# Four expert tiles with homes of their own beside the ring, and two block buffers in place of four

## The reference, cut to what matters

```python
def hier_moe(h, w_rg, b_rg, w_re, b_re, w1, w3, w2):
    ...
    slot_tok = jnp.zeros(n_blocks * MOE_BLOCK, jnp.int32).at[dest].set((order // TOP_K).astype(jnp.int32))
    ...
    xs = h[slot_tok].reshape(n_blocks, MOE_BLOCK, d_)

    def run(args):
        xb, e = args
        return (jax.nn.silu(xb @ w1[e]) * (xb @ w3[e])) @ w2[e]

    ys = lax.map(run, (xs, block_e)).reshape(-1, d_)
    return jnp.zeros_like(h).at[slot_tok].add(ys * slot_gate[:, None])
```

## Time and profile before

| | us |
|---|---|
| median of 3 runs | 2305.1 (2302.08 to 2305.42) |
| profiled execution | 2304.22 |
| its span | 2302.4 |
| PE busy | 2035.6 |
| DVE busy | 786.6 |
| ACT busy | 457.2 |
| POOL busy | 189.7 |

### The profile page before, as it was taken

How to read it: one execution, slowest core, us unless ns; L and a number is a source line. 1 busy time by engine, 2 the same in 40 slices (tenths; PEclk the granted TensorE clock), 3 DMA queues, 4 the chain that set the end, 5 groups by cost and what they waited for, 6 DMA issues and landing times.

```text
span 2302.4 us, 30476 instructions
## 1 busy us (share of the span) xinstructions
PE 2035.6 (88%) x11971; PEld 1212.3 (53%) x11972; DVE 786.6 (34%) x1836; ACT 457.2 (20%) x1059; POOL 189.7 (8%) x240
## 2 busy tenths in 40 slices
PE   6999999799877789999877777798999999999998
PEld 4566566444433335757433333344875575775574
DVE  1355674111111116656111111114466312456413
ACT  2142112111111112411111111111123212123112
POOL 1000001111111110001111111111000000000000
PEclk9999999999999999999999999999999999999999
DMA  9235649999999985686999999996343332343230
GB/s 376 110 129 240 255 156 378 423 426 427 427 425 426 425 345 211 236 317 257 424 425 425 424 425 425 427 420 242 134 182 129 111 147 110 147 165 129 95 142 19
DMA packets 62872, 640.95 MB, mean 278 GB/s; under 512 B 15868, under 2 KB 16420, under 8 KB 24240
## 3 DMA queue, kind: packets, MB, share of 16 engines
q1 hardware_dynamic: 41728, 588.39, 61.9%
q0 software_dynamic: 19984, 44.74, 5.5%
q10 hardware_dynamic: 1056, 6.37, 0.7%
HBM read 622.50 MB, written 44.17 MB: 290 GB/s over the span
## 4 chain that ended last, share of the span: by engine, by line
PE 62%; DMA 31%; DVE 4%; ACT 2%; issue 1%; SPq 0%; POOL 0%; DVEq 0%
DMA ring<-in_moe 26%; PE ps L866 10%; PE ps L1037 10%; PE ps L519 8%; PE ps L1051 6%; PE ps L1148 5%; PE ps L507 3%; PE ps L695 3%; DMA ring<-in_denseA 3%; PE ps L1220 2%; PE ps L872 2%; PE ps L1016 2%; PE ps L541 2%; PE ps L771 2%; PE ps L584 1%; DMA ring<-in_denseB 1%
## 5 line engine op out<-in xcount | busy, mean ns | idle before, releaser
L866 PE MATMUL ps<-ring,scr 128*64 128x256 f32 (+1 forms) x4800 | 667.5, 430 | 178.2 <-DMA ring<-in_moe 169.3
L866 PEld LDWEIGHTS ps<-ring,scr 128*64 128x64 f32 x4800 | 333.4, 138 | 485.9 <-DMA ring<-in_moe 239.3
L1833 DVE TENSOR_TENSOR scr<-ps,scr 128x512 f32<-128x512 f32 (+3 forms) x98 | 54.6, 558 | 574.6 <-PE ps L866 487.0
L1037 PE MATMUL ps<-ring,hT 128*128 128x512 f32 (+1 forms) x576 | 245.5, 578 | 5.1 <-ACT hT L1546 5.1
L519 PE MATMUL ps<-ring,hT 128*128 128x512 f32 (+1 forms) x512 | 199.3, 547 | 0.5 <-ACT hT L1516 0.5
L1444 POOL DMA_INDIRECT ys_scratch<-scr,ytab x128 | 125.0, 976 | 825.4 <-DVE scr L2495 791.6
L1670 ACT ACTIVATE scr<-ps 128x512 f32<-128x512 f32 x64 | 38.2, 597 | 760.8 <-PE ps L866 694.0
L2495 DVE COPY scr<-ps 128x1024 f32<-128x1024 f32 x64 | 78.4, 1224 | 269.3 <-PE ps L866 243.4
L1037 PEld LDWEIGHTS ps<-ring,hT 128*128 128x128 f32 x576 | 108.1, 193 | 117.8 <-issue 108.2
L1516 ACT ACTIVATE scr<-ps 128x256 f32<-128x256 f32 (+2 forms) x168 | 71.3, 436 | 403.7 <-PE ps L507 403.7
L519 PEld LDWEIGHTS ps<-ring,hT 128*128 128x128 f32 x512 | 97.3, 193 | 93.0 <-issue 89.2
(11 more groups left out here) (330 smaller groups left out, 2019.2 us busy)
## 6 DMA issues: line engine op xcount, KB each, us to landing
ring<-in_moe SPq DMA_DIRECT2D x192, 2048.0 KB, 15.9
ring<-in_denseB SPq DMA_DIRECT2D x48, 2048.0 KB, 7.7
ring<-in_denseA SPq DMA_DIRECT2D x36, 2048.0 KB, 16.2
scr<-ys_scratch POOLq DMA_DIRECT2D x6, 1024.0 KB, 7.2
modB<-mod_scratch POOLq DMA_DIRECT2D x10, 512.0 KB, 11.3
ring<-kv_scratch SPq DMA_DIRECT2D x2, 2048.0 KB, 8.6
tok_scratch<-hb POOLq DMA_DIRECT2D x6, 512.0 KB, 2.9
memT_scratch<-modB ACTq DMA_DIRECT2D x2, 1024.0 KB, 6.7
```

The costliest lines, as they stand in the source:

```text
L866: last = mm(out, lhs(c)[:, 0:64], w(c)[:, half * q:half * (q + 1)], start=(c == 0), stop=(c == n - 1))
L1037: last = mm(T["open"][:, 0:cols], hT16[:, c, t * P:(t + 1) * P], w[:, c, 0:cols], start=(c == 0), stop=(c == DC - 1))
L1833: return V.tensor_tensor(out, a, b, op)
```

## The change

Four expert tiles no longer pass through the ring. `ASIDE` lists their places: 3 in the first layer; 3, 7 and 10 in the second. Each has a home in memory that is idle at the time, in two halves of 1 MB that are loaded by two DMAs (`load_aside`). The others move up in the ring (`in_ring`), and SP's written-out part is one turn of its loop longer. In the first layer SP issues the aside tile after places 0 and 1 and after waits for the last router product's bank (`routed`), the modulation rows (rows_out) and the four writes of tokens (tok_out). In the second layer place 3 is issued ahead of place 0 (its wait, `turned`, is on transposes of the attention stage) and places 7 and 10 after `routed` and rows_out. The homes take half of `hb`, so the blocks have two buffers: gather k waits for block k - 2. In the second layer `xs_lo` and `xs_hi` are laid out for four blocks and not eight. PE's products and their order are the same; for an aside tile PE waits on its own semaphore.

```diff
-XS_W = SLOT_BLOCKS[0] * P + P
+XS_W = tuple(n * P + P for n in SLOT_BLOCKS)
+
+ASIDE = ((3,), (3, 7, 10))
...
-    xs_lo = hT[:, 0:3 * XS_W].rearrange("p (c t) -> p c t", c=3)
+    xs_lo = [hT[:, 0:3 * w].rearrange("p (c t) -> p c t", c=3) for w in XS_W]
...
-    xs_hi = cv(5, XS_W)
+    xs_flat = cv(5 * XS_W[0])
+    xs_hi = [xs_flat[:, 0:5 * w].rearrange("p (c t) -> p c t", c=5) for w in XS_W]
...
+    half_tile = TILE // 2
+
+    low_mod, low_rows = (v[:, 2:4, :].rearrange("p a b -> p (a b)") for v in (modB, hb))
+    aside = (((low_mod, low_rows),),
+             ((S[:, 2:4, :].rearrange("p a b -> p (a b)"), low_rows), (low_mod, hT[:, half_tile:2 * half_tile]),
+              (scr[:, 10400:10400 + half_tile], scr[:, 10400 + half_tile:10400 + 2 * half_tile])))
...
+    aside_in = [[sem(f"aside_in{l}_{j}") for j in ASIDE[l]] for l in range(DEPTH)]
...
-    SEG_M = 3 * E + 2
+    SEG_M = [3 * E + 2 - len(a) for a in ASIDE]
...
+    def in_ring(l, at):
+
+        return baseM[l] + at - sum(a < at for a in ASIDE[l])
+
     for l in range(DEPTH):
         for b in range(E):
             for k, s in enumerate((m_h1, m_h3, m_y)):
-                released[baseM[l] + place(b, k)] = (s, blocks_before[l] + b + 1)
+                if place(b, k) not in ASIDE[l]:
+                    released[in_ring(l, place(b, k))] = (s, blocks_before[l] + b + 1)
+    free_when = {}
...
+            free_when["turned", l] = (tp_full, T["tp"])
...
             route(nt - 1, 2)
+            free_when["routed", l] = (acc_free, T["acc"])
...
-                                                   hb[:, k % 4, c * P:(c + 1) * P], ident)
+                                                   hb[:, k % 2, c * P:(c + 1) * P], ident)
...
-            def moe_tile(i, q):
-
+            def moe_tile(i, at, width):
+
+                if type(i) is int and at in ASIDE[l]:
+                    n = ASIDE[l].index(at)
+                    pe.wait_ge(aside_in[l][n], 32)
+                    per = half_tile // width
+                    return lambda c: aside[l][n][c // per][:, c % per * width:(c % per + 1) * width]
+                q = in_ring(l, at) if type(i) is int else baseM[l] + at - len(ASIDE[l])
...
+            def load_aside(n):
+
+                src = d["moe"][l][tile_of(*in_order[ASIDE[l][n]])]
+                for k in range(2):
+                    sp_.dma_start(aside[l][n][k], src[:, k * half_tile:(k + 1) * half_tile]).then_inc(aside_in[l][n], 16)
+
+            def expert_tile(at):
+
+                dense(lambda i: d["moe"][l][tile_of(*in_order[at])], 1, in_ring(l, at))
+
+            if l > 0:
+                sp_.wait_ge(*free_when["turned", l])
+                load_aside(0)
+            expert_tile(0)
+            expert_tile(1)
+            sp_.wait_ge(*free_when["routed", l])
+            sp_.wait_ge(rows_out, (96, 144)[l])
+            if l == 0:
+                sp_.wait_ge(tok_out, 16 * 4)
+                load_aside(0)
+            else:
+                load_aside(1)
+                load_aside(2)
+            for at in range(2, 6 * UNROLL - 1):
+                if at not in ASIDE[l]:
+                    expert_tile(at)
+            with sp_.Fori(1, E // UNROLL - 1) as i:
...
-                if k >= 4:
-                    pool.wait_ge(rows_T, 2 * (K0 + k - 3))
-                pool.indirect_dma_start(hb[:, k % 4, :], None, tok_d,
+                if k >= 2:
+                    pool.wait_ge(rows_T, 2 * (K0 + k - 1))
+                pool.indirect_dma_start(hb[:, k % 2, :], None, tok_d,
```

More of the change, by code:

```diff
@@ L219, in program @@
     assert cv.at <= 4096, cv.at
+    half_tile = TILE // 2
[3 more added lines that the diff above has]
+              (scr[:, 10400:10400 + half_tile], scr[:, 10400 + half_tile:10400 + 2 * half_tile])))
+    assert 3 * XS_W[1] <= half_tile and 7168 + 5 * XS_W[1] <= 10400
     keys_new = lnB[:, :, :].rearrange("p a b -> p (a b)")
@@ L403, in program @@
         baseM.append(g)
-        g += SEG_M
+        g += SEG_M[l]
     for l in range(DEPTH):
@@ L815, in _ @@
             memory_keys(8 * DC - T["keys"])
-            B0, G0 = blocks_before[l], baseM[l]
+            B0 = blocks_before[l]
             pe.wait_ge(acc_free, T["acc"])
@@ L896, in work @@
                 def work(is_wide):
-                    w = moe_tile(i, G0 + (3 * u - 1 + k if u > 0 or type(i) is not int else k))
-                    products(2 * p + k, lambda c: w[:, c, :], DC, 512, lambda c: xgT[:, p, c, :],
+                    w = moe_tile(i, 3 * u - 1 + k if u > 0 or type(i) is not int else k, 512)
+                    products(2 * p + k, w, DC, 512, lambda c: xgT[:, p, c, :],
                              is_wide).then_inc((m_h1, m_h3)[k], 1)
@@ L920, in turn_gated, with down @@
                 either(flag, work)
-            def down(i, u, flag, q):
+            def down(i, u, flag, at):
                 p = u % 2
@@ L929, in work @@
                 def work(is_wide):
-                    w = moe_tile(i, q).rearrange("p (k n) x -> p k (n x)", n=2)
-                    products(6, lambda c: w[:, c, :], 4, D, lambda c: gT[:, p, c, :],
+                    w = moe_tile(i, at, D)
+                    products(6, w, 4, D, lambda c: gT[:, p, c, :],
                              is_wide).then_inc(m_y, 1)
@@ L954, in _ @@
                     pe.wait_ge(dest_ready, l + 1)
-                down(0, u - 1, before, G0 + 3 * u + 1)
+                down(0, u - 1, before, 3 * u + 1)
                 if beside:
@@ L967, in _ @@
                     up(i, u, 1, now)
-                    down(i, u - 1, before, G0 + 3 * u + 1)
+                    down(i, u - 1, before, 3 * u + 1)
             now = flag_of(0, E - 1)
             turn_gated(0, E - 1, now)
-            down(0, E - 1, now, G0 + 3 * E - 1)
+            down(0, E - 1, now, 3 * E - 1)
             o = ov[l]
-            slots = [(G0 + 3 * E + k) % RING for k in range(3)]
+            slots = [in_ring(l, 3 * E + k) % RING for k in range(3)]
             pe.wait_ge(dest_ready, l + 1)
@@ L1001, in _ @@
                     pe.wait_ge(o["y_copied"], j + 1)
-            mv_at = G0 + 3 * E
+            mv_at = in_ring(l, 3 * E)
             pe.wait_ge(mem_in, 16 * (2 * l + 2))
@@ L1304, in _ @@
                 dense(lambda i: tiles[i], SEG_A[l], baseA[l])
-            G0, B0 = baseM[l], blocks_before[l]
-            dense(lambda i: d["moe"][l][tile_of(*in_order[i])], 3 * UNROLL - 1, G0)
-            with sp_.Fori(0, E // UNROLL - 1) as i:
+            B0 = blocks_before[l]
+            def load_aside(n):
[21 more added lines that the diff above has]
+            with sp_.Fori(1, E // UNROLL - 1) as i:
                 for j in range(3 * UNROLL):
@@ L1639, in take_block @@
                 bank, c = ps[:, block_banks(k)[0], :], slice(k * P, (k + 1) * P)
-                A(xs_lo[:, :, c], bank[:, 0:384].rearrange("p (c x) -> p c x", c=3), ACT.Copy)
-                A(xs_hi[:, 0, c], bank[:, 384:512], ACT.Copy).then_inc(xs_act, 1)
+                A(xs_lo[l][:, :, c], bank[:, 0:384].rearrange("p (c x) -> p c x", c=3), ACT.Copy)
+                A(xs_hi[l][:, 0, c], bank[:, 384:512], ACT.Copy).then_inc(xs_act, 1)
             def blocks_taken(n):
@@ L1650, in expert_tokens @@
                 at = act.value_load(starts[0:1, index], min_val=0, max_val=SLOT_BLOCKS[l] * P)
-                A(xgT[:, p, 0:3, :], xs_lo[:, :, bass.ds(at, P)], ACT.Copy)
-                A(xgT[:, p, 3:8, :], xs_hi[:, :, bass.ds(at, P)], ACT.Copy).then_inc(done, 1)
+                A(xgT[:, p, 0:3, :], xs_lo[l][:, :, bass.ds(at, P)], ACT.Copy)
+                A(xgT[:, p, 3:8, :], xs_hi[l][:, :, bass.ds(at, P)], ACT.Copy).then_inc(done, 1)
             def gated_out(p, b):
@@ L2473, in _ @@
             dve.wait_ge(sc_full, T["sc"] - 4)
-            go(V.memset(xs_hi[:, :, end:end + P], 0.0))
-            go(V.memset(xs_lo[:, :, end:end + P], 0.0))
+            go(V.memset(xs_hi[l][:, :, end:end + P], 0.0))
+            go(V.memset(xs_lo[l][:, :, end:end + P], 0.0))
             done()
@@ L2481, in take_block @@
                 dve.wait_ge(rows_T, 2 * (K0 + k) + 2)
-                V.tensor_copy(xs_hi[:, 1:5, k * P:(k + 1) * P],
+                V.tensor_copy(xs_hi[l][:, 1:5, k * P:(k + 1) * P],
                               ps[:, block_banks(k)[1], :].rearrange("p (c x) -> p c x", c=4)).then_inc(xs_dve, 1)
```

11 lines of the change are left out of this document (6 added, 5 removed).

## The result

| | before | the change |
|---|---|---|
| median of 20 runs, us | 2304.33 (2300.33 to 2310.78) | 2309.49 (2302.81 to 2316.66) |
| ratio, 95% interval | | 1.0021 [1.0012, 1.0031] |
| profiled execution, us | 2304.22 | 2309.35 (span 2307.5) |

The change costs 5.2 us at the median. The interval of the ratio leaves out 1, so the small loss is real; 1.0021 is the very edge of what the forecast called no change, and its interval reaches to both sides of 0.2%; the time lies inside the range, some 4 us above the sum's +1.5. Behind the 5.2 stand two effects that are both larger and of opposite sign.

What follows compares the result with a forecast made beforehand. DMA bytes were taken to bound both expert stages (about 426 GB/s, 4.92 us per tile). First layer +11.1 and second -9.6 give +1.5 us on the profiled 2304.2, adjusted to the median and rounded to 2306 us; range 2299 to 2312.

Steps and rivals of the forecast that it cites:

- no change: Whole kernel: a time within about 0.2% (4.6 us) of before, 2300.5 to 2309.7 us; chance 0.45.
- the sum's +1.5: Both layers together: first layer +11.1 us and second layer -9.6 us give +1.5 us.
- The rival in which gather 6 comes in time: First layer: two full queues share bytes by halves, gather 6 lands by 402.5 us; total 2295.5 us, chance 0.27.
- slower rival: First layer: PE at half clock after gather 6 through the first up product, 6.6 us more; total 2311.7, chance 0.28.
- When gather 6 comes: First layer: gather 6 lands at 420.8 us behind POOL's other transfers, and PE waits some 15 us.
- +11 of the bounds 0 and 16: First layer: cost of PE's wait for gather 6, engines empty of tiles plus half clock, +11 us.
- 2.3 us of filling: First layer, after the wait: gather 7 and the next output writes fill some 2.3 us of the engines' empty time.
- The hole behind the aside tile: First layer: PE's use of the aside tile gives SP no new load, queue runs thin; +2.5 us, bounds 0 to 5.
- The moved gathers: Each layer: with two buffers, gathers of blocks 2 and 3 move into the full stretch, 1.05 MB, +2.5 us.
- Three tiles: Second layer: three expert tiles leave the full stretch at 4.92 us each, -14.8 us.
- the loop entry: Second layer: a hole can appear where PE enters the loop, +0.7 us, bounds 0 and 2.5.
- The early aside tile: Second layer: first aside tile slows the modulation rows' write ahead of the norm weights and routing, +2.0 us, bounds 0 to 4.9.

Runs made afterwards that it cites:

- e7: The change with two orders altered: first layer's second-norm loads behind gathers 6 and 7, second layer's first aside tile behind the routing; 2294.23 us, ratio 0.9951.
- e6: e5 plus an aside tile at place 3 of the first layer, homed outside hb, four block buffers kept there; 2292.6 us, ratio 0.9951.
- e9: The kernel of e6 measured once more, on one chip with e7; 2292.27 us, ratio 0.9941.
- e4: Against the kernel before: no aside tile at all, but two block buffers in both layers; 2324.09 us, ratio 1.0083.
- e5: The change with four buffers and no aside tile in the first layer, the second layer's three aside tiles all behind the routing; 2291.89 us, ratio 0.9948.

## Why the prediction was right, and where it was off

**The sign of each layer and the mechanism held.** Slower by a wait for gather 6 in the first, faster by three tiles in the second, no change that matters in the sum. The rival in which gather 6 comes in time fell, with its equal shares of two queues: the two lnB loads landed 6.9 us apart where 6.1 were taken and 2.5 would have been an equal share. Of the slower rival's 6.6 us of half clock, 2.7 came.

**The call of no change came out in part by luck.** The two layers were off the same way, by 3.0 and 1.2 us, and the median, 2309.49, lies 0.2 us inside the 2309.7 at which no change was to end. The prediction names two ranges, 2299 to 2312 and, under its numbers, 2293 to 2316; the time lies in both.

**When gather 6 comes: right, with two errors that cancel.** Counted from block 0's first turn it was forecast to land at 420.8 - 353.7 = 67.1 us and landed at 417.4 - 350.6 = 66.8. Gather 5 landed 1.7 us later than forecast (42.3 against 40.6), and from there to gather 6 it took 24.5 us in place of 26.5, for the two output writes were taken at 4.1 each and had landed 5.9 us after the second lnB load. The wait was forecast at some 15 us and was 15.92.

**What the wait costs: mis-sized.** This is the term "+11 of the bounds 0 and 16": 7.3 and 4.5 us without a tile, less 2.3 for what gather 7 and the next output writes would fill, and 1.5 for the clock. The window from 417.5 to 439 us gives 12.9, and the residue of the first layer, 14.1 less (-4.9 + 2.5 + 2.6), gives 13.9. Here is the same stretch cut at the issue of the lone tile (425.0 us) and at its landing (432.7), and then the queues' packets and MB in the whole of it:

```profile
417.50:425.00 7.50, 7.44 (x25) 3.23 (x26) 0.71 (x2) 1.82 (x4) 0.00 (x0) 0.62 0.08 30
425.00:432.70 7.70, 4.60 (x30) 3.06 (x31) 1.81 (x2) 0.66 (x2) 1.94 (x2) 0.83 0.78 277
432.70:439.00 6.30, 6.30 (x54) 3.63 (x53) 0.59 (x1) 2.14 (x4) 0.00 (x0) 0.94 0.58 192
```

```profile
q1 hardware_dynamic: 232, 3.38, 44.9%
q0 software_dynamic: 336, 0.17, 2.7%
```

At 426 GB/s these lose 7.5 x 396 / 426 = 7.0 us, 7.7 x 149 / 426 = 2.7 and 6.3 x 234 / 426 = 3.5, 13.1 in all, net of whatever any queue moved. The forecast, cut at the same points, had 4.5 + 1.5 = 6.0 up to the issue, 2.8 for what a lone tile takes beyond its transfer, and 1.7 + 2.8 = 4.5 behind it: 13.3, from which the 2.3 went off. So the hole was sized about right, and **the 2.3 us of filling is the term that was off**. POOL's queue moved 0.17 MB there, 0.4 us: gather 7 and the writes of expert 1 had gone, all but 0.16 MB, while the engines were still full, and the two writes of expert 2 were small (0.02 MB in 425 to 433 us). Inside the 13.1 two errors cancel: the first piece is 1.0 longer, for the half clock took 0.85 + 1.85 = 2.7 us ahead of the release where 1.5 was allowed, and the last is 1.0 shorter.

The clock is read from the granted clock behind the wait, in the change (5 us) and then in e7 (3.4 us, after a wait of 2.91 us), as in rows 9:

```profile
417.50:422.50 5.00, 4.94 (x16) 2.57 (x18) 0.69 (x1) 1.82 (x4) 0.00 (x0) 0.50 0.12 44
```

```profile
407.60:411.00 3.40, 3.37 (x12) 2.10 (x14) 0.69 (x1) 1.82 (x4) 0.00 (x0) 0.50 1.02 427
```

It is the half level, 1.2 GHz, both times. In the change it fell while PE stood still: 1.00 in 401.6 to 405.0 us, 0.50 in 407.0 to 417.5. In e7 it costs nothing that can be seen in bytes, for the engines are full. The slower rival had PE at this level through all of the turn, the down product, block 7 and the first up product. The turn was (1.94 us), the down product only in part (5.50, where the rival had 7.3); the turn of block 7 took 1.09 us, the first up product 5.36 as before. The time is nearer to the rival's 2311.7 than to 2306, but the clock has 1.2 us in that and the filling that did not come 1.9.

**The hole behind the aside tile: right.** Taken at +2.5, measured 2.6; in e6 2.1 and in e9 3.2. **The moved gathers: right**, 2.5 against 2.8 (e4).

**The second layer: -9.6 against -8.4.** Three tiles -14.8 and two gathers +2.5, with 0.7 for the loop entry, make -11.6 for the stage; measured -10.7. The hole there was nearer 1.3, since e4 gives 13.5 for the three tiles. The early aside tile was put at +2.0; the norm weights came 2.3 us later after the large product (174.3 against 172.0) and the first turn too. The first is shown by eight kernels without it, the second may be scatter, as said under e5. The DMA share stayed 1.01 at 424 GB/s through this stage, so the reading that bytes bound it held.

**The sum.** 14.1 - 8.4 = +5.7 for the parts that the change touches, against +1.5. The front and the rest, -3.1 and +2.5 in this one execution, nearly cancel.

## What to carry to other kernels

When buffers are taken from a queue that issues in order, list what stands behind the instruction that will now wait: here two loads needed much later moved in front of the one transfer that PE was about to need, and moving them behind it was worth 0.6%. This stage, bound by bytes, lost nothing while its consumer stood still (422 GB/s), but when the queue of loads then ran dry: price such a wait by the time from the last tile's landing to the next release, the clock included, plus what a lone load takes beyond its transfer (7.7 us against 4.9 here). Take off for other queues only what they will still have to move in that hole (0.17 MB here, where 1 MB was assumed). When a small transfer shares the engines with a queue of large ones, compare packets and not bytes. A tile taken out of a full ring is worth its transfer only if the releases around it stay dense (4.5 of 4.9 us in the second layer, 1.2 to 2.7 in the first).

## What the runs showed of the hardware

- A 512 KB load on POOL's queue beside a full queue of 2 MB loads takes 6 to 7 us of that queue: 6.9 between the two lnB landings here, 6.1 and 6.2 in rows 5 and 6. The two queues moved about equally many packets (596 and 621, 594 and 593, 501 and 499 in three kernels), while their bytes were 8.63 and 1.65 MB in the first of these.
- The eight transfers of POOL's queue followed here, from gather 5 on, landed in the order of issue but for one pair: 418.7 us for a write issued at 395.7, 420.5 for the gather issued at 394.4.
- PE's granted clock went to the half level after a wait of 2.91, 3.18 or 15.92 us alike, and the work that followed was about equally slow: 1.94 us for the turn of a block in place of 1.09, 5.5 to 5.7 for a down product in place of 3.65. A wait five times as long cost no more of the clock.
- A tile whose queue is otherwise empty lands 7.7 us after its issue (425.0 to 432.7 us in the change), as is the median of the in_denseB loads; its 2.10 MB would take 4.9 at 426 GB/s.
